# Row-norm sums as two rounded products, one tile later, with the next weights rounded ahead of the first squares or silu

## The reference

```
def rms_norm(x, g):
    y = x * rsqrt(mean(x * x, axis=-1) + EPS)
    return y * g

def macaron_half(x, g, w_in, w_out):
    a, b = split(rms_norm(x, g) @ w_in, 2, axis=-1)
    return x + 0.5 * ((silu(a) * b) @ w_out)
```

## Time and profile before

| | us |
|---|---|
| median of 3 runs | 1274.79 |
| the profiled execution | 1274.76 |
| its span in the profile | 1272.9 |
| TensorE matmuls busy | 1262.3 |
| VectorE busy | 751.5 |
| ScalarE busy | 561.8 |
| GpSimd busy | 188.1 |

### The profile page before, as it was taken

How to read it: one execution, slowest core, us unless ns; L and a number is a source line. 1 busy time by engine, 2 the same in 40 slices (tenths; PEclk the granted TensorE clock), 3 DMA queues, 4 the chain that set the end, 5 groups by cost and what they waited for, 6 DMA issues and landing times.

```text
span 1272.9 us, 22412 instructions
## 1 busy us (share of the span) xinstructions
PE 1262.3 (99%) x8780; PEld 1243.4 (98%) x8780; DVE 751.5 (59%) x1131; ACT 561.8 (44%) x829; POOL 188.1 (15%) x208
## 2 busy tenths in 40 slices
PE   9999999999999999999999999999999999999999
PEld 9999999999998999999999999999997899999999
DVE  7766575555676656564554775554456756656433
ACT  6543453343375533433343443433355764343322
POOL 0120021146144000000132000001134410000000
PEclk9999999999999999999999999999999999999999
DMA  8464445643204443444453534454441134343343
GB/s 302 139 180 139 162 150 165 216 166 132 100 34 136 159 163 134 165 164 141 146 176 112 197 133 149 148 165 161 155 169 34 67 133 166 133 163 134 134 140 129
DMA packets 38829, 187.46 MB, mean 147 GB/s; under 512 B 4432, under 2 KB 13136, under 8 KB 23664
## 3 DMA queue, kind: packets, MB, share of 16 engines
q1 hardware_dynamic: 37296, 183.25, 41.8%
q0 software_dynamic: 1184, 3.13, 1.2%
q10 hardware_dynamic: 288, 0.24, 0.1%
HBM read 179.70 MB, written 6.90 MB: 147 GB/s over the span
## 4 chain that ended last, share of the span: by engine, by line
PE 94%; DVE 2%; ACT 2%; DMA 1%; issue 1%; POOL 0%; SPq 0%; DVEq 0%; ACTq 0%
PE bank L504 29%; PE bank L506 29%; PE bank L505 29%; PE bank L741 1%; PE bank L780 1%; PE bank L783 1%; DVE wlo L1559 1%; DMA raw<-in_w_ffn_in 1%; PE bank L750 1%; ACT whi L1154 1%; PE bank L918 0%; DMA x<-in_xT 0%; PE outs L530 0%; POOL mixlo L2208 0%; PE outs L817 0%
## 5 line engine op out<-in xcount | busy, mean ns | idle before, releaser
L504 PE MATMUL bank<-xhi,whi 128*128 128x320 f32 (+1 forms) x1760 | 546.3, 310 | 0.9 <-DVE wlo L1940 0.7
L506 PE MATMUL bank<-xhi,wlo 128*128 128x320 f32 (+1 forms) x1760 | 543.2, 309 | 0.0
L505 PE MATMUL bank<-xlo,whi 128*128 128x320 f32 (+1 forms) x1760 | 543.2, 309 | 0.0
L1559 DVE TENSOR_TENSOR wlo<-raw,whi 128x2048 fp32r<-128x2048 f32 (+1 forms) x176 | 361.7, 2055 | 236.9 <-ACT whi L1154 236.7
L1154 ACT ACTIVATE whi<-raw 128x2048 fp32r<-128x2048 f32 (+1 forms) x177 | 304.5, 1721 | 326.6 <-PE bank L506 324.4
L504 PEld LDWEIGHTS bank<-xhi,whi 128*128 128x128 f32 x1760 | 330.8, 188 | 3.6 <-issue 2.5
L505 PEld LDWEIGHTS bank<-xlo,whi 128*128 128x128 f32 x1760 | 330.9, 188 | 0.5
L506 PEld LDWEIGHTS bank<-xhi,wlo 128*128 128x128 f32 x1760 | 330.7, 188 | 0.0
L504 PE MATMUL bank<-hhi,whi 128*128 128x320 f32 x704 | 217.8, 309 | 0.0
L506 PE MATMUL bank<-hhi,wlo 128*128 128x320 f32 x704 | 217.5, 309 | 0.0
L505 PE MATMUL bank<-hlo,whi 128*128 128x320 f32 x704 | 217.5, 309 | 0.0
(11 more groups left out here) (235 smaller groups left out, 1056.4 us busy)
## 6 DMA issues: line engine op xcount, KB each, us to landing
raw<-in_w_ffn_in SPq DMA_DIRECT2D x85, 1024.0 KB, 4.8
raw<-in_w_ffn_out SPq DMA_DIRECT2D x64, 704.0 KB, 4.1
raw<-in_w_in_a SPq DMA_DIRECT2D x10, 1024.0 KB, 4.8
raw<-in_w_out SPq DMA_DIRECT2D x8, 1024.0 KB, 4.8
raw<-in_w_kv SPq DMA_DIRECT2D x6, 1024.0 KB, 4.8
raw<-in_w_mkv SPq DMA_DIRECT2D x4, 1024.0 KB, 4.8
raw<-in_w_in_b SPq DMA_DIRECT2D x4, 1024.0 KB, 4.8
raw<-in_w_ffn_in SPq DMA_DIRECT2D x6, 256.0 KB, 6.2
```

The costliest lines, as they stand in the source:

```text
L504: mm(acc, wh, mhi(ks[q]), start=start and q == 0, stop=False)
L505: mm(acc, wh, mlo(ks[q]), start=False, stop=False)
L506: last = mm(acc, wl, mhi(ks[q]), start=False, stop=stop and q == nk - 1)
L1559: tt(wlo[slot][:, 0:size], raw[slot][:, 0:size], f32(whi[slot][:, 0:size]), ALU.subtract).then_inc(lo_ready[slot], 1)
```

## The change

Two new tiles ssum_hi and ssum_lo hold ssum rounded to fp32r and the rest; ones_hi holds the 1/1024 matrix in fp32r (1/1024 is exact in it). ScalarE writes ssum_hi (`sum_hi_of`), GpSimd then subtracts it (`sum_rest`, at the end of each `add_squares` and first in its queue for in0), and TensorE's `row_norm` becomes two fp32r matmuls, each with its own wait. In pa, in1, kv, pb and in3 it is issued behind the second tile of the stage; in0 and mkv0 keep the place. In ScalarE's order of pa, in1, kv, pb and in3, the rounding of slot 0's next block moves from behind the first tile's square or silu to directly behind the inverse root, before any square, table load or silu of the stage. For mkv0 the rounding of the sums stands behind in0's last instruction and the table load.

```diff
--- before.py
+++ after.py
@@ -244,6 +244,9 @@
         cmk = sb("cmk", [P, 2, N_MEM])
         cmv = sb("cmv", [P, 2, N_MEM])
         ssum = sb("ssum", [P, R])
+        ssum_hi = sb("ssum_hi", [P, R], F32R)
+        ssum_lo = sb("ssum_lo", [P, R], F32R)
+        ones_hi = sb("ones_hi", [P, P], F32R)
         r = sb("r", [P, R])
 
 
@@ -303,6 +306,8 @@
         xn_lo = sem("xn_lo")
         sq_ready = sem("sq_ready")
         ssum_step = sem("ssum_step")
+        sum_hi = sem("sum_hi")
+        sum_lo = sem("sum_lo")
         ms_ready = sem("ms_ready")
         root = sem("root")
         r_ready = sem("r_ready")
@@ -508,10 +513,12 @@
 
             def row_norm(stage, w):
                 g = NORM[stage]
-                pe.wait_ge(ssum_step, KD * (g + 1))
+                pe.wait_ge(sum_hi, g + 1)
                 if g >= 1:
                     pe.wait_ge(r_ready, g)
-                mm(MS[:, 0:w], ones_d[:].broadcast_to([P, P]), ssum[:, 0:w], start=True, stop=True).then_inc(ms_ready, 1)
+                mm(MS[:, 0:w], ones_hi[:], ssum_hi[:, 0:w], start=True, stop=False)
+                pe.wait_ge(sum_lo, g + 1)
+                mm(MS[:, 0:w], ones_hi[:], ssum_lo[:, 0:w], start=False, stop=True).then_inc(ms_ready, 1)
 
             def wait_acc(t, depth=4):
                 if not isinstance(t, int) or t >= depth:
@@ -561,7 +568,7 @@
                         f += 1
                 return f
 
-            def projection(stage, w, groups, tiles, xin=(xhi, xlo), norm_at=0, after=None, before=None, within=None):
+            def projection(stage, w, groups, tiles, xin=(xhi, xlo), after=None, before=None, within=None):
 
                 n0, t0, x0 = PAIR0[stage], TILE0[stage], XN0[stage]
                 for j in range(tiles):
@@ -593,7 +600,7 @@
                         product(banks[(t0 + j) % 4][:, 0:w], slot, col, 256, range(KD), KD,
                                 lambda k: xin[0][:, k, 0:w], lambda k: xin[1][:, k, 0:w], True, True, each
                                 ).then_inc(acc_ready, 1)
-                    if j == norm_at and stage in NORM:
+                    if j == (0 if stage == "mkv0" else 1) and stage in NORM:
                         row_norm(stage, w)
                     for hn, first, lag in groups:
                         if 0 <= j - lag - first < HNORM[hn][1]:
@@ -647,7 +654,7 @@
                         product(banks[4 + j if spare else j][:, 0:R], slot, col, 256, range(KD), KD,
                                 lambda k: xhi[:, k, :], lambda k: xlo[:, k, :], True, True, each
                                 ).then_inc(acc_ready, 1)
-                        if first and j == 0 and stage in NORM:
+                        if first and j == 1 and stage in NORM:
                             row_norm(stage, R)
                         if after:
                             after(j)
@@ -1177,8 +1184,13 @@
                 roots[0] += 4
                 last_root[:] = [out_sem, n]
 
+            def sum_hi_of(stage, w):
+                act.wait_ge(ssum_step, KD * (NORM[stage] + 1))
+                nc.scalar.activation(ssum_hi[:, 0:w], ssum[:, 0:w], ACT.Copy).then_inc(sum_hi, 1)
+
             def row_norm(stage, w):
                 if stage not in ("in0", "mkv0"):
+                    sum_hi_of(stage, w)
                     nc.scalar.preload_act_table_set("natural_log_exp_and_others")
                 act.wait_ge(ms_ready, NORM[stage] + 1)
                 inverse_root(MS[:, 0:w], P, w, r_ready, NORM[stage] + 1)
@@ -1211,13 +1223,16 @@
                 nxt = block_size(NEXT[stage])
                 if early_split:
                     split_hi(0, n0 + 1, nxt, acc_ready, t0 + 2)
+                ahead = stage in NORM and not early_split
                 if stage in NORM:
                     row_norm(stage, w)
+                if ahead:
+                    split_hi(0, n0 + 1, BLK, acc_ready, t0 + 2)
                 for j in range(tiles):
                     if before:
                         before(j)
                     pair, slot, col = j // 4, (j // 2) % 2, j % 2
-                    if col == 1 and not (late_split and j >= tiles - 3) and not (early_split and j == 1) and not (
+                    if col == 1 and not (ahead and j == 1) and not (late_split and j >= tiles - 3) and not (early_split and j == 1) and not (
                             stage == "kv" and j == tiles - 1):
                         size = BLK if pair < tiles // 4 - 1 else nxt
                         split_hi(slot, n0 + pair + 1, size, acc_ready, t0 + j + 1)
@@ -1233,15 +1248,17 @@
             def ffn_in(stage, after=None):
                 n0, t0 = PAIR0[stage], TILE0[stage]
                 m0 = {"in0": 0, "in1": KF, "in2": 2 * KF, "in3": 3 * KF}[stage]
-                if stage in NORM and stage != "in0":
+                ahead = stage in NORM and stage != "in0"
+                if ahead:
                     row_norm(stage, R)
+                    split_hi(0, n0 + 1, BLK, acc_ready, t0 + 2)
                 nc.scalar.preload_act_table_set("silu_and_others")
 
                 def body(i, size):
                     for c in range(2):
                         act.wait_ge(acc_free, t0 + 4 * i + c + 1)
                         nc.scalar.activation(silu[:, c, :], gate[:, c, :], ACT.Silu).then_inc(silu_out, 1)
-                        if c == 0 and not (stage == "in0" and isinstance(i, int) and i == 0):
+                        if c == 0 and not ((stage == "in0" or ahead) and isinstance(i, int) and i == 0):
                             split_hi(0, n0 + i + 1, BLK if size is None else size, acc_ready, t0 + 4 * i + 2)
                     for c in range(2):
                         if c == 1 and not (stage == "in0" and isinstance(i, int) and i == 0):
@@ -1255,7 +1272,9 @@
                     for i in range(4):
                         body(i, None)
                         after(i)
-                with act.Fori(4 if after else 0, 10) as i:
+                elif ahead:
+                    body(0, None)
+                with act.Fori(4 if after else 1 if ahead else 0, 10) as i:
                     body(i, None)
                 body(10, block_size(NEXT[stage]))
 
@@ -1437,6 +1456,7 @@
             act.dma_start(raw[1][:, 0:256], weights["in0"][1][:, 0:256]).then_inc(d_piece1[0], 16)
             nc.scalar.preload_act_table_set("natural_log_exp_and_others")
             act.wait_ge(d_early, 16)
+            nc.scalar.activation(ones_hi[:], ones_d[:].broadcast_to([P, P]), ACT.Copy)
             for q, (k0, k1) in enumerate(START):
                 own = slice(256 * k0, 256 * k1)
                 act.wait_ge(d_x[q], 16)
@@ -1454,6 +1474,7 @@
             act.wait_ge(d_third, 16)
             act.wait_ge(first_half, 1)
             nc.scalar.activation(whi[0][:, 0:BLK // 2], raw[0][:, 0:BLK // 2], ACT.Copy).then_inc(third_hi, 1)
+            sum_hi_of("in0", R)
             act.wait_ge(landed[0], 16 * (PAIR0["in0"] + 1) + 16)
             act.wait_ge(acc_ready, TILE0["in0"] + 2)
             nc.scalar.activation(whi[0][:, BLK // 2:BLK], raw[0][:, BLK // 2:BLK], ACT.Copy).then_inc(hi_ready[0], 1)
@@ -1471,6 +1492,7 @@
 
             ffn_in("in0", lambda i: memory_in(i - 1) if i else None)
             nc.scalar.preload_act_table_set("natural_log_exp_and_others")
+            sum_hi_of("mkv0", N_MEM)
             act.wait_ge(acc_ready, TILE0["mkv0"])
             for k in range(KD):
                 input_hi(memt[:, k, :], xhi[:, k, 0:N_MEM], "mem1", k)
@@ -2124,6 +2146,12 @@
 
         @block.gpsimd
         def _(pool):
+            def sum_rest(g, w):
+
+                pool.wait_ge(sum_hi, g + 1)
+                nc.gpsimd.tensor_tensor(ssum_lo[:, 0:w], ssum[:, 0:w], ssum_hi[:, 0:w].bitcast(F32), ALU.subtract
+                                        ).then_inc(sum_lo, 1)
+
             def add_squares(g, w):
 
                 for k in range(KD):
@@ -2137,6 +2165,7 @@
                         pool.wait_ge(ssum_step, s)
                         nc.gpsimd.tensor_tensor(ssum[:, 0:w], ssum[:, 0:w], sq[:, k % 2, 0:w], ALU.add
                                                 ).then_inc(ssum_step, 1)
+                sum_rest(g, w)
 
             def head_squares_lo(hn, src, w, written, count, tiles=None):
 
@@ -2241,6 +2270,7 @@
                 return run_memory_first if layer else run_heads_first
 
 
+            sum_rest(0, R)
             pool.wait_ge(landed[0], 32)
             for dst, src in const_loads:
                 pool.dma_start(dst[:], src).then_inc(d_const, 16)
```

## The result

The changed kernel takes 1296.04 us (median of four runs, 1295.86 to 1297.11), against 1274.67 for the one before on the same chip: a ratio of 1.0171 with a 95% interval of 1.0159 to 1.0184. It is slower by 21.4 us where 11.4 was forecast. The direction is right, the time lies 6 us above the range. The profiled execution has a span of 1294.3 us, 21.4 more than in the earlier trace rows, so its trace can be read for the difference.

What follows compares the result with a forecast made beforehand. TensorE was taken to bound the kernel. Stalls of 13.17 us plus 0.77 for having waited, less 2.25 saved and 0.32 regained, gave +11.4 us: 1286.2 us, range 1282 to 1290.

Steps and rivals of the forecast that it cites:

- the savings: At the seven norms, two fp32r matmuls replace the fp32 one and waits in in1 and in3 go: 2.25 us saved.
- the stalls of in0 (+0.9 against +0.7) and mkv0: TensorE waits for late rounded sums: 1.16 us in in0, 0.32 of it regained, and 2.3 in mkv0 behind a table load.
- in1 and in3 at nothing: Norms of in1 and in3: a 0.43 us stall each against 0.55 saved each; predicted shift 0.
- the large term: First head statistic behind tile 2 comes late: stalls of 3.44 us in pa and in kv, 1.97 in pb.
- VectorE's end + 0.74: A GpSimd subtraction running beside VectorE's wlo ends 0.74 us after VectorE does, as seen in pa.
- A rule weighed: Skill page's full lockout: the late GpSimd subtraction would need 0.88 us after VectorE, sum 0.7 higher; 0.74 was kept.
- though GpSimd's clearing of qz ... then starts 4 us later, just done when it is next needed.: In pa, the 4.37 us clearing starts 4 us later behind the new sums; no stall was expected there.
- They now start at 169 instead of 73 and end at 174 ... Covered by 1.5 us.: GpSimd's eight scratch writes and constant chain, behind mkv0's wait, would end before mkv0's head squares at 175.5.
- the idle here is cut in two by the hi matmul, and 1.3 us did not do it.: Argument against the clock falling in the new stalls; the longest earlier idle, 1.3 us, brought no change of step.
- The clock rival: TensorE's clock halves after stalls in mkv0, pa, kv and pb: 8.7 us on top, 1294.9 us; chance 0.06.
- the main case: Stalls as summed at all places, +11.4 us, giving 1286.2 us; chance 0.80.
- no weight is late at these places now: At the norms, the moved rounding of weights gives no saving, being no TensorE work and no weight being late.

Runs made afterwards that it cites:

- The two experiments on order: Changed kernel with the rounding back behind tile 0's square in pa, kv, pb: 1289.58 us; changed kernel with wlo held until the first hsq_lo is done: 1289.29 us.
- the products alone: Changed kernel with the norm back behind the first tile and the roundings back in their old places, leaving the two rounded products: 1304.70 us.
- the kernel filled in pa and kv alone: Changed kernel with scratch writes ahead of mkv0's ssum_lo and unread matmuls filling only pa's and kv's stalls: 1288.87 us.
- the first experiment: Changed kernel with mkv0's ssum_lo made behind the eight scratch writes in GpSimd's order, so these are issued early again: 1293.07 us.
- the experiment on the place alone: Kernel before, with only the float32 norm moved behind the second tile in pa, in1, kv, pb and in3: 1279.57 us, ratio 1.0039.

## Why the prediction was right, and where it was wrong

Right: the bound (TensorE, with every stall a loss), the savings (the two products 0.15 apart), the stalls of in0 (+0.9 against +0.7) and mkv0 (2.1 against 2.2, before its slow steps), in1 and in3 at nothing, and the large term. In kv the wait is 0.71 + 2.25 and the shift without slow steps is 3.2, against a forecast of 3.3; in pb 1.7 against 1.8. The two experiments on order show its cause to be the one given. "VectorE's end + 0.74" held: in kv the wlo ends at 680.45, the subtraction at 681.17, 0.72 later, and not the 0.88 of "A rule weighed".

Wrong, in three steps, which together are the missing 10 us:

- *"though GpSimd's clearing of qz ... then starts 4 us later, just done when it is next needed."* The step asked when GpSimd was next wanted, not who works beside it. VectorE's scaling of idd waited 4.25 us, and behind it in VectorE's queue stood rt, on the path to the head statistic. Cost: 2.0 us in the trace (pa's shift of 7.6, less 2.3 of slow steps, against 3.3), and 2.0 by experiment, the latter with other differences that happened to cancel. The row for the scaling in the trace before (1.03 us for 64 columns, behind another operation on 64 columns that takes 0.22) would have given it away.
- *"They now start at 169 instead of 73 and end at 174 ... Covered by 1.5 us."* This counted the time in which GpSimd issues the eight writes, not the transfers: in the new place three of the eight are still on their way, and a fourth just landing, when out0's first load is issued at 180.5. Cost: 2.9 us at out0 in the trace, 3.0 by experiment. As the load lands when it lands, much of what TensorE loses ahead of it in mkv0 is lost only once: out0's stall and mkv0's slow steps together are 4.4, and in the four traces where the slow steps were absent and the writes late the stall was 3.9 to 4.5.
- *"the idle here is cut in two by the hi matmul, and 1.3 us did not do it."* The clock rival, at 0.06, came true beside the main case. One matmul between two stalls did not keep the clock up in pa and kv, nor in mkv0 in this execution. Cost: 5.3 us in the trace, 1.5 in mkv0 and 3.8 in pa and kv; of the 3.8 an experiment gave back 3.4 to 4.2. The rival's price was too high (8.7 for four places; three fell, for 1.5 to 2.3 each), and it should have been a term of the sum and not an alternative: a stall and what follows it do not exclude one another.

2.0 + 2.9 + 5.3 is 10.2, where the measured change exceeds the forecast by 10.0; the other terms together came out 0.2 lower.

What decides whether the clock falls is not settled here. It fell at 2.15 + 2.69, at 0.71 + 2.25, at all five norms of the products alone (0.50 + 2.00 and 0.23 + 2.27 the shortest), at one wait of 1.94 (in two of four executions, by their mean granted clock) and at waits of 3.0 to 4.5 at out0. It did not fall at pb's 1.71, nor at out0's 2.90 in the changed kernel. In mkv0 it fell at 1.28 + 0.45 in two traces and not in three; at 1.28 + 0.84 it fell in the trace of the kernel filled in pa and kv alone and not in the first experiment's, two kernels that do the same up to there. The Trainium skill, page "TensorE: Matmul & The Clock Gate", Part 1, says that the number of slow matmuls at a kernel's start varies from run to run of one kernel. The traces here agree on the variation, and show it in the middle of a kernel, down to none.

A smaller omission showed in the experiments: the prediction named no use for the rounding in front of the silu, beyond "no weight is late at these places now". In the new place of the norm one would be late by 1.1 us in in1 and in3, as the experiment on the place alone shows.

## What to carry to other kernels

When an instruction is moved or made to wait, list everything behind it in its queue, and ask three questions of each: who works beside it at the new time (a shared port), what its transfers share the DMA engines with, and when its own engine is next wanted; the first cost 2 us here, the second 3, the third about 2 in an experiment. Price a stall of TensorE as long as those of 2 us and more here with the slow steps behind it as well (1.1 to 2.4 us), as a risk and not as a certainty. Where a kernel is so close to its limits, compare executions with the same granted clock. And a cheaper instruction whose operands must first be made by two other engines is worth only what it saves (0.3 us a norm) if these engines have time there: the saving must be set against the late start, place by place.

## What the runs showed of the hardware that was not expected

- GpSimd's MEMSET, which reads no tile, holds VectorE's scaling of a 128x64 fp32 tile for its whole length: 4.25 us beside it, 0.25 without. Of VectorE's two-input wlo and a GpSimd subtraction started after it, the first grew from 2.29 to 2.63 at most and the second from 0.87 to 2.79. The Trainium skill, page "SBUF — State Buffer", section "Who interferes with whom", names tensor_scalar among the operations that can take the shared ports and be blocked for a whole instruction; the trace agrees.
- Eight writes of 72 KB each from GpSimd's queue took up to 14 us to land, and stretched a 704 KB load on another queue from 4.0 us to 9.4. Issued over 28 us, away from that load, they took 9 at most and the load its 4.0 (the kernel was 3.0 us faster).
- Waits of TensorE under 3 us could make the granted clock fall to half: 1.94 in one piece in some executions, 0.71 + 2.25 with a matmul between. But 2.90 in one piece did not, in one trace. Each fall made 9 to 20 matmuls slow, at a cost of 1.1 to 2.4 us. Unread matmuls in the gaps of pa and kv kept it at 1.00, and that was worth 3.4 to 4.2 us.
